# Windowed attention beside a delta rule: from a loop of its own into the levels of the delta steps

## The chip, the cores and the metric

One core of one Trainium2 chip runs the whole program. The metric is the time of one execution in microseconds (us), measured on the device. A core has five engines with an in-order queue each: TensorE (PE: matrix products, and transposes as products with the identity), VectorE (DVE), ScalarE (ACT), GpSimd (POOL) and SyncE (SP), which only issues transfers here. They meet at semaphores only. TensorE writes to PSUM, eight banks of 512 float32 per partition. All numbers are float32; a large product is made of three products of split operands (high and low part), a small one runs in float32 itself, in two passes (so a "x8" in the profile is four matmuls).

## The reference, cut to what matters

Two layers of a transformer trunk over 128 prompt tokens (tile 0) and 512 sample tokens (tiles 1 to 4), 1024 features. The change is in the even layer, whose mixer has two parts side by side behind one input projection and in front of one output projection:

```
s_ctx = einsum("bqgrd,bkgd->bgrqk", q_i, k_ctx) * scale       # window attention of the sample tiles
s_loc = where(valid, einsum("bqgrd,bkgd->bgrqk", q_i, k_i) * scale, -inf)
m = max(max(s), sink); e = exp(s - m); p = e / (sum(e) + exp(sink - m))
oa = p_ctx @ v_ctx + p_loc @ v_i                              # 8 heads of 64, 2 groups of keys
ob, s_f, s_b = delta_bidir(q, k, v, g, beta, s0_f, s0_b)      # 4 heads, forwards and backwards
ob = rmsnorm(ob, out_norm) * silu(gate)
out = concatenate([oa, ob]) @ w_out
```

A prompt tile attends to its own 128 keys. A sample tile attends to its own tile, its neighbours (masked to a window of 128) and 128 cached keys: three key tiles for sample tiles 1 and 4, four for tiles 2 and 3. The reference solves a triangular system per chunk of the delta rule; the kernel does that by doubling.

## The kernel before

The even layer runs in stages. **Input projection**: 23 column blocks of 128, each 48 matmuls; after the last ones the keys and values of the delta rule are turned (`kv_turn`, L2266). **Delta steps** (`for r in range(NT)`, L2390 on PE, L1664 on DVE, L998 on ACT): five steps, each for one tile forwards and one backwards (c = 0 and 1, both in flight), the fifth for the prompt tile. A step makes the decayed Gram matrix, then inverts it in levels: at each level lv = 1 to 5, PE makes Z for both directions (L2418), DVE multiplies Z by that level's mask (`level_z`, L1705), PE makes two products of it ("TR", L2471 and L2474), and DVE adds these into `r_blocks` and `t_blocks` (the level's sums, L1711, L1714). A level needs the sums of the one before. Behind the levels come a last Z and TR (L2496, L2510), V = R times beta v (L2528), the outputs and the new state. Between these, PE has filler: the adaLN map of the other sub-layers, 40 pieces of 1 MB of `w_mod`, whole (L2212) or in two halves (L2221), eight a step, through four buffers (`MSLOTS = 4`), issued by SP, one behind another; the rotation of one of five rows of q and k a step (`rope_swap_a`, L2364, with `rotated_a` on DVE, L1628 to L1636); and `k_times_state` (L2386) at levels 4 and 5, with `v_beta` on DVE (L1661) behind it.

**Attention** (L2612 on PE, L1800 on DVE, L1088 on ACT) starts when the last delta step has ended: 40 units of one tile and one head. Per unit: scores (PE, L2577, two heads at once), scores plus mask and the row maximum in one instruction (DVE, L1806), its negative (L1810), exp with the row sum (ACT, L1095), exp of the sink (L1097), transposes of the probabilities (PE, L2202), their copy (ACT, L500), values (PE, L2600), sum, reciprocal and scaling (DVE, L1785 to L1791). Scores, transposes and values have two PSUM banks each. Between units lie the norm and gate of the delta output (`on_step`, `on_stat`), the split of attention output into high and low part per tile, `gains`, the first two splits of `w_out`, and `keep_busy` (L2207), products that nobody reads. **Output projection** (`out_halves(0)`, L2081) waits for all of it: its first two column blocks have their weights by then, blocks 2 to 7 are split from ACT's `out_split` (L1115) and DVE (L1464) on.

The order on each engine is written out by hand; nothing reorders it.

Of the kernel before, what the change touches and what calls it, by code (L numbers as in the profile page):

```python
# [109 lines left out]
def build(nc, a, outs):  # L110
# [21 lines left out]
    NORMS = (("first", KD, 1), ("l2", 8, 8), ("on", 4, 8), ("cq", C_Q // P, 1), ("ckv", C_KV // P, 1))  # L132
# [162 lines left out]
    MSLOTS = 4  # L295
# [3 lines left out]
    MROW = place("mod_rows", [512], R_T + 4 * al(TW))  # L299
    SM = [place(f"scores{s}", [512], R_F + 1024 + 512 * s) for s in range(2)]  # L300
    PR = [place(f"probs{s}", [512], R_F + 2048 + 512 * s) for s in range(2)]
    PT = [place(f"probs_t{s}", [512], R_F + 3072 + 512 * s) for s in range(2)]
    ASM = place("attn_small", [256], R_F + 4096)
    OA = [place(f"o_attn{s}", [512], R_F + 512 * s) for s in range(2)]
# [154 lines left out]
    ALLU = [(t, c + 4 * g2) for t in ATT for c in range(4) for g2 in range(2)]  # L459
    A_ROPE = (4, 0, 1, 2, 3)  # L460
    ON_AT = [4 + 8 * h for h in range(B_HEADS)]

    def on_head(u, step):

        return ON_AT.index(u - step) if u - step in ON_AT else None
# [26 lines left out]

    def att_copy_a(act, u):

        t, h = ALLU[u]
        c0, c1 = att_local(t)
        act.wait_ge(S("a_turned"), u + 1)
        if u >= 2:
            act.wait_ge(S("a_pv"), u - 1)
        act.activation(PT[u % 2][:, c0:c1], PS[:, 1024 + 512 * (u % 2) + c0:1024 + 512 * (u % 2) + c1], ACT.Copy  # L500
                       ).then_inc(S("a_pt"), 1)


# [60 lines left out]
    with stack:  # L564
# [4 lines left out]
        def _(sp):  # L569
# [43 lines left out]
            for n in range(23):  # L613
                if n < E_AB:
                    load(n, ein_v[:, :, (6 + n) * P:(7 + n) * P])
                elif n == E_AB:
                    load(n, ein_v[:, :, 22 * P:22 * P + 16])
                    sp.dma_start(CT[:, C_FOUR, 0:16], consts[:, C_FOUR, 0:16]).then_inc(S("consts_landed"), 16)
                    for dst, name in ((DTB, "ev_dt_bias"), (EAL, "ev_a_log")):
                        src = a[name][0].rearrange("(o d) h -> o (d h)", o=1).broadcast_to([P, 8])  # L620
                        sp.dma_start(dst[:, :], src).then_inc(S("side_landed"), 16)
                elif n < E_QA + 4:
                    load_two(n, [ein_v[:, :, 64 * h:64 * h + 64] for h in (n - E_QA, n - E_QA + 4)])
                else:
                    c = n - E_QA if n < E_GATE else n - 1
                    load(n, ein_v[:, :, c * P:(c + 1) * P])
            sp.dma_start(CT[:, C_AMASK:, :], consts[:, C_AMASK:, :]).then_inc(S("consts_landed"), 16)
# [130 lines left out]
        def _(act):  # L758
# [184 lines left out]
            def k_rows(t):  # L943
                act.wait_ge(S("kv_turned"), 2 * t + 1)
                act.activation(KTOK[:, t, :, :], q4(bank(4 + 2 * (t % 2))), ACT.Copy).then_inc(S("k_tok"), 1)
# [51 lines left out]

            for r in range(NT):  # L998
                for c in range(2):
# [6 lines left out]
                    act.activation(DQ[c][:, :, :], DQ[c][:, :, :], ACT.Exp, scale=-1.0).then_inc(S("d_exp"), 1)  # L1006
                for c in range(2):
# [28 lines left out]
                if r == 0:  # L1036
                    act.wait_ge(S("va_turned"), 2)
                    act.activation(AV[:, 4, :], bank(7, P), ACT.Copy).then_inc(S("v_rows"), 1)
                for c in range(2):
# [11 lines left out]
            o_copy(NT - 1, 0)  # L1051


            def on_step(u):

                h = on_head(u, 0)
                if h is not None:
                    if h == 0:
                        for c in range(2):
                            act.wait_ge(*both("o_done", c, NT))  # L1060
                    if h >= 2:
                        act.wait_ge(*of("stat", "on", 2 * (h - 1)))
                    act.activation(ONSQ[h % 2][:, :], OD[:, h, :], ACT.Square).then_inc(S("norm_sq"), 1)
                for hf in range(2):
                    cs = slice(hf * HW, hf * HW + HW)
                    h = on_head(u, 2 + 2 * hf)
                    if h is not None:
                        act.wait_ge(*of("stat", "on", 2 * h + hf + 1))
                        if h >= 2:
                            act.wait_ge(S("on_gated"), 2 * (h - 1))  # L1070
                        act.activation(ONRL[h % 2][:, cs], bank(7, HW), ACT.Ln, scale=1.0 / P, bias=EPSC[:, 0:1]
                                       ).then_inc(S("norm_ln"), 1)
                    h = on_head(u, 3 + 2 * hf)
                    if h is not None:
                        act.wait_ge(*of("ln", "on", 2 * h + hf + 1))
                        act.activation(ONRL[h % 2][:, cs], ONRL[h % 2][:, cs], ACT.Exp, scale=-0.5).then_inc(S("norm_rstd"), 1)
                h = on_head(u, 8)
                if h is not None:
                    act.wait_ge(S("on_gated"), 2 * h + 2)
                    act.activation(Hh[:, 4 + h, :], OD[:, h, :], ACT.Copy).then_inc(S("on_hi"), 1)  # L1080

            def att_out(i, sem):

                t = ATT[i]
                act.wait_ge(S("oa_turned"), i + 1)
                act.activation(Hh[:, 0:4, TILES[t]:TILES[t] + P], q4(bank(6)), ACT.Copy).then_inc(S(sem), 1)

            for u, (t, h) in enumerate(ALLU):  # L1088
                s = u % 2
                c0, c1 = att_local(t)  # L1090
                act.wait_ge(S("a_max"), u + 1)
                if u >= 2:

                    act.wait_ge(S("a_turned"), u - 1)
                act.activation(PR[s][:, c0:c1], SM[s][:, c0:c1], ACT.Exp, bias=ASM[:, 64 + u:65 + u],  # L1095
                               scale=A_HD ** -0.5, accum_out=ASM[:, 128 + u:129 + u]).then_inc(S("a_exp"), 1)
                act.activation(ASM[:, 192 + u:193 + u], SNK[:, h:h + 1], ACT.Exp, bias=ASM[:, 64 + u:65 + u]  # L1097
                               ).then_inc(S("a_sink"), 1)
                if u >= 1:
                    att_copy_a(act, u - 1)  # L1100
                if u in (2, 3):
                    if u == 2:
                        act.wait_ge(S("mod_done"), KD + MPARTS)
                    hi(N0_EVEN_OUT + u - 2)
                on_step(u)
                if u % 8 == 3 and t != ATT[0]:
                    att_out(ATT.index(t) - 1, "oa_hi")
            att_copy_a(act, len(ALLU) - 1)
            att_out(NT - 1, "oa_hi")
# [45 lines left out]
            act.wait_ge(S("on_lo"), B_HEADS)  # L1155
# [178 lines left out]
        def _(dve):  # L1334
# [261 lines left out]
            step(dve.scalar_tensor_tensor(EB[:, :], EB[:, :], -1.0, BETA[:, :], ALU.mult, ALU.mult), "gates_ready")  # L1596
            w_rest(E_GATE + 2)
            for t in range(NT):
                if t == 2:
                    w_rest(E_GATE + 3)  # L1600
                dve.wait_ge(S("kv_turned"), 2 * t + 2)
                dve.tensor_copy(VTOK[:, t, :, :], q4(bank(5 + 2 * (t % 2)))).then_inc(S("v_tok"), 1)
# [5 lines left out]
            def mod_rows(i):  # L1608

                dve.wait_ge(S("mod_done"), KD * (i + 2))  # L1610
                dve.tensor_copy(MROW[:, :], bank(6)).then_inc(S("mod_rows"), 1)

# [4 lines left out]
            def mod_out(i):  # L1617
# [3 lines left out]
                mod_columns(l, m0 // P, 7, "mod_cols")  # L1621

            def rope_a(r, part):

                dst = QA[:, A_ROPE[r], S0:S0 + SAMPLE]
                if part == 0:
                    dve.wait_ge(S("a_swapped"), r + 1)
                    dve.tensor_tensor(ROTA[:, :], bank(7), CT[:, C_SIN:C_SIN + 4, :].rearrange("p a b -> p (a b)"), ALU.mult  # L1628
                                      ).then_inc(S("a_rotated"), 1)
                elif part == 1:  # L1630
                    dve.tensor_tensor(dst, dst, CT[:, C_COS:C_COS + 4, :].rearrange("p a b -> p (a b)"), ALU.mult
                                      ).then_inc(S("a_cosine"), 1)
                else:
                    dve.wait_ge(S("a_rotated"), r + 1)
                    dve.wait_ge(S("a_cosine"), r + 1)
                    dve.tensor_tensor(dst, dst, ROTA[:, :], ALU.add).then_inc(S("a_roped"), 1)  # L1636
# [18 lines left out]
            def v_minus(r, c):  # L1655
# [6 lines left out]
                last.then_inc(S("v_minus"), 1)  # L1662

            for r in range(NT):  # L1664
# [28 lines left out]
                last.then_inc(S("level_ready1"), 1)  # L1693

# [1140 lines left out]
```

## Time and profile before

| | us |
|---|---|
| median of 3 runs | 1902.68 (1900.95 to 1903.35) |
| the profiled execution, its own time | 1901.23 |
| its span | 1899.4 |
| PE busy | 1808.8 (95%) |
| DVE busy | 988.6 (52%) |
| ACT busy | 816.0 (43%) |
| delta steps, 226 to 435.7: PE, DVE, ACT busy of 209.7 | 187.3, 117.1, 51.5 |
| attention, 435.7 to 530: PE, DVE, ACT busy of 94.3 | 83.1, 65.9, 66.3 |

Start times are counted from the span's start. "Idle before" in brackets is the time that the engine stood idle ahead of the instruction, and who ended it; "issue" means that no semaphore explains it. PEclk 1.00 is TensorE's 2.4 GHz, 0.50 its 1.2 GHz. Matmuls overlap, so for PE the distance between starts says what a group costs.

### The profile page before, as it was taken

How to read it: one execution, taken by the hardware profiler on the slowest of the kernel's cores; microseconds unless marked ns; L12 is line 12 of the kernel's file. 1: busy time of each engine (PE TensorE's matmuls, PEld its weight loads, DVE VectorE, ACT ScalarE, POOL GpSimd, SP SyncE). 2: the span in 40 equal slices, each digit the busy share in tenths (PEclk: the TensorE clock that was granted, in tenths of full speed). 3: DMA queues.
4: the chain of work that ended last, by engine and by line, in shares of the span. 5: the costliest groups of instructions: out<-in, count | busy, mean ns of one | idle time of the engine just before them, and what ended most of it. 6: DMA issues, size and time to landing. Idle time of an engine off the chain costs nothing. (4 is left out here: it accounts for less than half of the span.)

```text
span 1899.4 us, 36570 instructions
## 1 busy us (share of the span) xinstructions
PE 1808.8 (95%) x14803; PEld 1667.0 (88%) x14803; DVE 988.6 (52%) x1838; ACT 816.0 (43%) x1396; POOL 55.8 (3%) x57
## 2 busy tenths in 40 slices
PE   5999989988899999999999999999999999999998
PEld 3999867667799999999999887776899999999997
DVE  4443345656747655235556843344376553355555
ACT  4545422225745544124445654343455442243453
POOL 0000222220000000000000000000000000000000
PEclk9999999999999999999999999999999999999999
DMA  7232376751021222222234311011211232122243
GB/s 289 67 69 57 122 222 214 214 178 57 1 72 45 78 74 86 72 67 74 70 99 140 94 49 31 24 33 31 67 45 56 77 89 78 56 77 77 81 135 117
DMA packets 244627, 170.25 MB, mean 90 GB/s; under 512 B 20922, under 2 KB 231068, under 8 KB 243356
## 3 DMA queue, kind: packets, MB, share of 16 engines
q1 hardware_dynamic: 244508, 168.55, 29.8%
q8 instruction: 88, 1.44, 0.3%
q14 instruction: 31, 0.25, 0.0%
HBM read 165.09 MB, written 3.44 MB: 89 GB/s over the span
## 5 line engine op out<-in xcount | busy, mean ns | idle before, releaser
L769 ACT ACTIVATE w_hi<-w_raw 128x1024 fp32r<-128x1024 f32 (+4 forms) x186 | 197.7, 1063 | 529.2 <-PE ps L2003 416.1
L1351 DVE TENSOR_TENSOR w_lo<-w_raw,w_hi 128x1024 fp32r<-128x1024 f32 (+4 forms) x190 | 233.0, 1227 | 346.9 <-ACT w_hi L769 346.5
L2003 PE MATMUL ps<-h_hi,w_hi 128*128 128x320 f32 x1632 | 373.9, 310 | 4.4 <-ACT conv L1178 2.4
L2003 PE MATMUL ps<-h_hi,w_lo 128*128 128x320 f32 x1632 | 371.8, 309 | 0.0
L2003 PE MATMUL ps<-h_lo,w_hi 128*128 128x320 f32 x1632 | 371.7, 309 | 0.0
L2003 PEld LDWEIGHTS ps<-h_hi,w_hi 128*128 128x128 f32 x1632 | 272.8, 188 | 6.5 <-ACT conv L1178 2.9
L2003 PEld LDWEIGHTS ps<-h_lo,w_hi 128*128 128x128 f32 x1632 | 273.0, 188 | 0.0
L2003 PEld LDWEIGHTS ps<-h_hi,w_lo 128*128 128x128 f32 x1632 | 272.8, 188 | 0.0
L2081 PE MATMUL ps<-g_hi,w_hi 128*128 128x320 f32 x352 | 110.1, 313 | 3.2 <-DVE g_lo L1850 2.0
L2081 PE MATMUL ps<-g_lo,w_hi 128*128 128x320 f32 x352 | 108.8, 309 | 0.0
L2081 PE MATMUL ps<-g_hi,w_lo 128*128 128x320 f32 x352 | 108.8, 309 | 0.0
L1357 DVE SCALAR_TENSOR_TENSOR conv<-u,vec_cols,conv 128x511 f32<-128x511 f32 x200 | 101.3, 548 | 14.4 <-ACT conv L1178 11.6
L1361 DVE SCALAR_TENSOR_TENSOR conv<-u,vec_cols,conv 128x511 f32<-128x511 f32 x200 | 100.7, 546 | 0.0
L2081 PE MATMUL ps<-h_hi,w_out_hi 128*128 128x320 f32 x288 | 90.4, 314 | 0.1
L2081 PE MATMUL ps<-h_hi,w_out_lo 128*128 128x320 f32 x288 | 89.0, 309 | 0.0
L2081 PE MATMUL ps<-h_lo,w_out_hi 128*128 128x320 f32 x288 | 89.0, 309 | 0.0
L1183 ACT ACTIVATE g_hi<-gated 128x640 f32 (+1 forms) x44 | 32.6, 742 | 105.1 <-DVE gated L1848 105.1
L2081 PEld LDWEIGHTS ps<-g_hi,w_hi 128*128 128x128 f32 x352 | 66.1, 188 | 4.5 <-DVE g_lo L1850 2.5
L1178 ACT ACTIVATE conv<-ps,vec_cols 128x640 f32<-128x640 f32 x88 | 69.3, 787 | 0.0
L2081 PEld LDWEIGHTS ps<-g_lo,w_hi 128*128 128x128 f32 x352 | 66.1, 188 | 0.2
L2081 PEld LDWEIGHTS ps<-g_hi,w_lo 128*128 128x128 f32 x352 | 66.1, 188 | 0.0
L1868 DVE COPY f_t<-ps 128x640 f32 (+1 forms) x16 | 13.2, 825 | 98.3 <-PE ps L2003 80.5
(364 smaller groups left out, 3299.6 us busy)
## 6 DMA issues: line engine op xcount, KB each, us to landing
w_raw<-in_ffn_w_up SPq DMA_DIRECT2D x88, 512.0 KB, 3.8
w_mod_raw<-in_w_mod SPq DMA_DIRECT2D x80, 512.0 KB, 4.5
w_raw<-in_ffn_w_down SPq DMA_DIRECT2D x48, 704.0 KB, 4.6
w_raw<-in_ev_w_in SPq DMA_DIRECT2D x18, 512.0 KB, 3.8
w_mod_first<-in_w_mod SPq DMA_DIRECT2D x8, 1024.0 KB, 15.8
w_raw<-in_ev_w_out SPq DMA_DIRECT2D x8, 512.0 KB, 4.7
w_raw<-in_od_w_out SPq DMA_DIRECT2D x8, 512.0 KB, 4.1
w_raw<-in_od_w_kv_up SPq DMA_DIRECT2D x24, 128.0 KB, 2.3
```

What stands on the lines that cost most here:

```text
L769: act.activation(WH[slot][:, 0:k, :], RAW[slot][:, 0:k, :], ACT.Copy).then_inc(w_hi, 1)
L1178: act.activation(halves(Y[b][:, :]), pair(b0 + 2 * slot), ACT.Copy, scale=vcol(v0 + b * FCH, j)).then_inc(evac_a, 1)
L1183: act.activation(row(Gh, j), GP[:, :], ACT.Copy).then_inc(S("g_hi_written"), 1)
L1351: dve.tensor_tensor(WL[slot][:, 0:k, :], RAW[slot][:, 0:k, :], WH[slot][:, 0:k, :].bitcast(F32), ALU.subtract).then_inc(w_lo, 1)
L1357: dve.scalar_tensor_tensor(y[:, c0 + 1:c1], u[:, c0:c1 - 1], w_before, y[:, c0 + 1:c1], ALU.mult, ALU.add).then_inc(S(signal), 1)
L1361: dve.scalar_tensor_tensor(y[:, c0:c1 - 1], u[:, c0 + 1:c1], w_after, y[:, c0:c1 - 1], ALU.mult, ALU.add).then_inc(S(signal), 1)
L1868: dve.tensor_copy(halves(row(F, m)), pair(2 * slot)).then_inc(evac_v, 1)
L2003: last = pe.matmul(out, w_of(k, wi), x_of(k, xi, i), start=(k == 0 and p == 0), stop=(k == ks - 1 and p == 2))
L2081: last = pe.matmul(out, w[wi][:, k, :], x[xi][:, k, tk(g)], start=(k == 0 and p == 0), stop=(k == ks - 1 and p == 2))
```

## The change

- The attention loop is gone. Its work stands in the delta steps: tile r's attention in step r. A sample tile has four pairs of heads (q = 0 to 3, one head of each key group). On PE, pair q's scores are behind level q's TR, its transposes (head by head, both through bank 7) around level q + 2's TR, its values in level q + 3, in front of TR. DVE's `pair_max` for pair q stands behind the sums of level q + 1. The prompt tile is one batch of eight heads in step 0.
- There is one set of score banks (2 and 5), so pair q + 1's scores wait for pair q's maximum. The probabilities are written over the masked scores. Sinks, sums, reciprocals and scaling are done once a tile (`normalise`). TR's results move from banks B and C to A and B.
- `k_times_state` moves from levels 4 and 5 to levels 0 and 1 in steps 1 to 3, with `v_beta`.
- The rotations move into the projection's last blocks (one `rope_swap_a` behind each of blocks 18 to 22), for which the constants are loaded earlier; `kv_turn` has three banks instead of four.
- `MSLOTS` falls from 4 to 3, to make room.
- Behind the steps: the delta output's norm (one root over both halves a head), the splits of eight chunks of the output projection's input, one after another in the order `TAIL`, and the first two column blocks, whose products are interleaved chunk by chunk as these come. `keep_busy` is gone there.

The diff's core, in this order: buffers, ACT in a step, DVE's `pair_max` and its place, PE in a level of steps 1 to 4 (TR lies at the third line of dots), `att_scores`, ACT behind the steps (DVE follows it chunk by chunk).

```diff
-    MSLOTS = 4
+    MSLOTS = 3
+    S_BANK, O_BANK, O_AT = (2, 5), (1, 4), 128
+    TAIL = (0, 1, 2, 4, 3, 5, 6, 7)
...
+                att_exps(r, 0)
+                for q in range(pairs(r)):
+                    att_pt_copy(r, q, 0)
+                    if q + 1 < pairs(r):
+                        att_exps(r, q + 1)
+                    else:
+                        att_sink(r)
+                    att_pt_copy(r, q, 1)
...
+            def pair_max(r, q):
+                p, u = batch(r, q), 8 * r + 2 * q
+                c0, c1 = att_local(r)
+                dve.wait_ge(S("a_scores"), p + 1)
+                if p >= 2:
+                    dve.wait_ge(S("a_turned"), 2 * (p - 1))
+                for g2 in range(2):
+                    last = dve.tensor_tensor_reduce(SM[p % 2][:, g2, c0:c1], PS[:, 512 * S_BANK[g2] + c0:512 * S_BANK[g2] + c1],
+                                                    CT[:, C_AMASK:C_AMASK + 4, :].rearrange("p a b -> p (a b)")[:, c0:c1],
+                                                    1.0, SNK8[:, q + 4 * g2:q + 4 * g2 + 1], ALU.add, ALU.max, ASM[:, u + g2:u + g2 + 1])
+                last.then_inc(S("a_rowmax"), 1)
+                dve.wait_ge(S("a_rowmax"), 5 * r - 2 + q)
+                neg_max(u, 2)
...
+                    if 0 < r < NT - 1 and lv == 1:
+                        v_minus(r, 1)
+                    if r > 0 and lv < 5:
+                        pair_max(r, lv - 1)
...
+                    else:
+                        if lv < 4:
+                            mod_first_half(r, lv + 2)
+                        if lv == 1 and r < NT - 1:
+                            k_times_state(r, 1)
+                        if lv > 2:
+                            for c in range(2):
+                                pe.wait_ge(*both("t_written", c, t0 + lv))
+                            att_values(r, lv - 3)
+                        if lv > 1:
+                            att_turn(r, lv - 2, 0)
...
+                        if lv < 4:
+                            mod_piece(r, lv + 2, halved=True)
+                        if lv > 1:
+                            att_turn(r, lv - 2, 1)
+                        if lv < 4:
+                            att_scores(r, lv)
...
+            def att_scores(r, q):
+                if q:
+                    pe.wait_ge(S("a_rowmax"), 5 * r - 3 + q)
+                else:
+                    for c in range(2):
+                        pe.wait_ge(*(both("kq_copied", c, r + 1) if r < 2 else both("o_done", c, r)))
...
+            on_square(0)
+            att_hi(0)
+            hi(N0_EVEN_OUT)
+            on_square(1)
+            on_root(0)
+            hi(N0_EVEN_OUT + 1)
+            att_hi(1)
+            on_square(2)
+            on_root(1)
+            att_hi(2)
+            on_square(3)
+            on_out(0)
+            att_hi(3)
+            on_root(2)
+            on_out(1)
+            on_root(3)
+            on_out(2)
+            on_out(3)
```

## Rows read from the trace of the kernel before

**Rows 1.** The page: busy time of TensorE, and the transfers of `w_mod`.
```profile
PE 1808.8 (95%) x14803; PEld 1667.0 (88%) x14803; DVE 988.6 (52%) x1838; ACT 816.0 (43%) x1396; POOL 55.8 (3%) x57
...
w_mod_raw<-in_w_mod SPq DMA_DIRECT2D x80, 512.0 KB, 4.5
```

**Rows 2.** Stretches, busy time by engine: projection's end, last TR to `w_out`, blocks 0 and 1.
```profile
200.00:219.00 19.00, 19.00 (x138) 18.99 (x137) 3.12 (x4) 3.82 (x6) 0.00 (x0) 1.00 0.00 1
...
434.40:529.59 95.19, 83.95 (x676) 66.24 (x676) 67.16 (x270) 65.93 (x192) 0.00 (x0) 1.00 0.06 18
529.59:536.70 7.11, 7.11 (x48) 7.11 (x49) 2.69 (x3) 3.49 (x6) 0.00 (x0) 1.00 0.37 110
```

**Rows 3.** Stretches, level 1's TR to V in steps 1, 2, 3, 4 (same columns).
```profile
281.96:306.26 24.30, 21.21 (x574) 15.19 (x571) 12.20 (x43) 1.66 (x4) 3.79 (x4) 0.93 0.74 227
325.11:345.73 20.62, 19.71 (x575) 14.16 (x571) 12.07 (x42) 1.67 (x4) 5.12 (x5) 1.00 0.77 232
365.18:388.69 23.51, 20.34 (x575) 14.27 (x571) 12.05 (x42) 1.66 (x4) 4.50 (x5) 1.00 0.71 223
408.14:428.64 20.50, 18.12 (x559) 12.47 (x555) 10.20 (x34) 1.66 (x4) 4.51 (x5) 1.00 0.51 160
```

**Rows 4.** TensorE in time, step 2, level 2: start, duration, engine, line.
```profile
326.75 1.15 PE L2418 MATMUL ps<-r_blocks,a_blocks 64*64 64x64 f32 x32
327.83 0.64 PE L2221 MATMUL ps<-w_mod_raw,silu_c 128*32 128x256 f32 x8
328.40 0.25 PE L2471 MATMUL ps<-level_z,t_blocks 64*64 64x32 f32 x2
...
329.46 0.64 PE L2221 MATMUL ps<-w_mod_raw,silu_c 128*32 128x256 f32 x8
330.03 1.13 PE L2364 MATMUL ps<-qa_ka_va,consts 128*128 128x512 f32 x2
...
335.45 1.16 PE L2386 MATMUL ps<-state,qkv_b 128*128 128x128 f32 x8
```

**Rows 5.** VectorE in time, the last of the same level's sums.
```profile
329.80 0.28 DVE L1714 TENSOR_TENSOR t_blocks<-t_blocks,ps 128x128 f32<-128x128 f32 x1
```

**Rows 6.** TensorE in time, attention units of four key tiles.
```profile
457.84 0.71 PE L2577 MATMUL ps<-qa_ka_va 64*128 64x128 f32 x8
...
458.93 0.66 PE L2202 MATMUL ps<-consts,probs 128*128 128x128 f32 x4
459.42 1.00 PE L2600 MATMUL ps<-v_attn_tok,probs_t 128*128 128x64 f32 x8
```

**Rows 7.** VectorE and ScalarE in time, units of 512 columns.
```profile
454.62 0.75 DVE L1806 CUSTOM_DVE_ANT_0 scores<-ps,consts,sink_scaled 128x512 f32<-128x512 f32 x1 [1.35 <-issue]
...
455.41 0.15 DVE L1810 TENSOR_SCALAR attn_small<-attn_small 128x1 f32<-128x1 f32 x1
...
455.60 0.72 ACT L1095 ACTIVATE probs<-scores,attn_small 128x512 f32<-128x512 f32 x1 [1.81 <-DVE attn_small L1810]
...
458.18 0.58 ACT L500 ACTIVATE probs_t<-ps 128x512 f32<-128x512 f32 x1
```

**Rows 8.** In time: a whole-row copy on ScalarE; then a group of its lines.
```profile
467.34 0.72 ACT L1080 ACTIVATE h_hi<-o_delta 128x640 fp32r<-128x640 f32 x1
...
L1769 DVE TENSOR_TENSOR h_lo<-o_delta,h_hi 128x640 fp32r<-128x640 f32 x4 | 3.3, 818 | 0.0
...
L1126 ACT ACT_TABLE_LOAD x1 | 1.3, 1283 | 0.0
```

**Rows 9.** TensorE alone: length, busy (instructions), granted clock, DMA share, GB/s.
```profile
282.99:284.99 2.00, 0.00 (x0) 1.00 0.54 152
286.40:289.80 3.40, 3.40 (x80) 0.50 0.67 208
231.00:233.00 2.00, 0.00 (x0) 1.00 0.77 217
...
238.70:245.50 6.80, 5.85 (x116) 0.50 0.65 199
```

## What the change does to the time

> **What bounds the kernel now.** The page first: TensorE is busy for 95% of the span [rows 1], so a stage is read by what PE does in it. The stretches by stage come next. The end of the input projection is solid PE, 19.00 of 19.00 us [rows 2]. The delta steps are nearly so: from level 1's TR to V step 2 takes 20.6 us with 19.7 busy; steps 1, 3 and 4 take 24.3, 23.5 and 20.5 [rows 3]. In time, a level is Z (1.08 us from start to start), half a `w_mod` piece (0.57), TR (1.06) and the other half (0.57), and DVE's sums end 1.6 us after TR began [rows 4, 5]; so a level without more costs 3.3 us, and what is put into it costs its own PE time. Behind the steps, 95.2 us pass from the last delta product to the first product of the output projection, and another 7.1 for that projection's blocks 0 and 1: 102.3 us until block 2 starts [rows 2]. PE, DVE and ACT are there busy for 84, 66 and 67 us: none is full, the units go round a chain PE, DVE, ACT, PE, ACT, PE.
>
> **The tail (gain).** What is left behind the steps hangs on ACT. From the last delta product: output copies to +1.4 us, then on ACT 4 squares, 4 attention chunks, 4 delta chunks (640 columns, about 0.63 apart by the 0.72 of [rows 8]), 2 weight splits (0.95 each) and 4 roots (Ln and Exp with a wait between, 1.45), the last two estimated by their length from the same kind of passes: 2.5 + 2.5 + 2.5 + 1.9 + 5.8 = 15.2 us, to +16.6. The last head's gate (two DVE passes, 0.9 each), its copy (0.7) and its low part (0.82, [rows 8]) come behind its root, which ends at +15.5: +19.9. ACT's splits of block 2 wait for that: table load 1.3 [rows 8], split 1.05, DVE 1.25: block 2 starts at +23.6. PE's blocks 0 and 1, interleaved by chunk, need only 0.9 us behind the last chunk and are hidden in this. 102.1 (to 434.4, the last product's end) less 23.6 is **-78.5**. Bounds: if the chunks come as DVE's queue allows and no faster, +26 (-76); if the roots cost 1.2, +22.5 (-79.6). Behind it the splits of blocks 4 to 7 have a cycle of 6.9 us for two (load 4.7, 1.0, 1.2) against PE's 7.0: no cover is left, no cost yet.
>
> **The projection (loss).** A rotation's product costs PE 1.06 us [rows 4]. Four are moved from the steps to a stage that is solid PE: 4.2; the fifth falls where PE waits for ACT's last evacuation, free. Three banks for `kv_turn` cost two short waits for copies, 0.6. **+4.9**, between 4.2 and 6. The steps' side of this move is in the sums below. DVE's 2 us a rotation lie beside, in a stretch where it is 3.1 of 19.0 busy [rows 2].
>
> **A level with attention, four key tiles (steps 2 and 3).** Per pair PE adds: scores 1.09, two turns 0.49 each, values 2 x 0.91 [rows 6]. All times below from TR's start. DVE is through with the sums at 1.6; `pair_max` is two instructions 0.79 apart [rows 7]: 3.2. PE is through with TR, half piece and turn at 2.1 and waits for the maximum, since there is one set of score banks: 1.1 us idle. Then scores, Z, half piece.
> - Level 2 to 3: 3.2 + 1.09 + 1.08 + 0.57 + values 1.82 + turn 0.49 = 8.2.
> - Level 3 to 4: no half piece, and the values wait for the second turn's copy. That copy stands on ACT behind the next pair's exps: maximum 3.2, its negative 0.15, two exps 0.72 apart, copy 0.58 [rows 7], 0.1 for hand-overs: 5.5. Then 1.82 + 0.49 = 7.8.
> - Level 4 to 5: no scores left. PE has TR, turn, Z until 2.6 and waits for the same copy until 5.5: 2.9 us idle. 7.8.
> - Level 1 to 2: `v_beta` (four products, 1.0 in the same timeline) stands on DVE in front of `pair_max`: maximum at 4.2, PE ready at 1.6: 2.6 us idle. 4.2 + 1.09 + 1.08 + 0.57 + 0.49 = 7.45.
> - Level 5 to V: TR 1.06, turn, last Z 0.61, whole piece 0.9, values, TR 0.61, whole piece 0.9 = 6.4. `normalise` is beside V.
>
> Sum 37.7. In front of level 1's TR stand one `k_times_state` (1.1, [rows 4]) and scores more, and the second `k_times_state`: +3.2; that both left levels 4 and 5 is in the comparison. Step 2: 37.7 + 3.2 - 20.6 = **+20.3**. Step 3 (23.5 before; its own first levels were held by DVE's `o_add`, so only +2.5 in front): **+16.7**.
>
> **Three key tiles (steps 1 and 4).** PE's part times 3/4, maxima 0.66 and exps 0.61 apart, copy 0.47: 6.9 + 7.2 + 6.7 + 6.7 + 5.8 = 33.2, idle 2.3, 1.0, 0.9 and 2.4 us. Step 1: 33.2 + 3.0 - 24.3 = **+11.9**. Step 4 has no `v_beta` (32.2); the first scores wait for `o_add` (+1.0), and `normalise` delays v_new by 0.55 since no `gc_rows` covers it: 32.2 + 1.6 - 20.5 = **+13.3**.
>
> **Step 0 (the prompt).** Scores 1.2, turns 0.9, values 1.8 on PE less the rotation 1.1. The scores and the row maximum fall into two waits of PE for `w_mod`, of which 231.00:233.00 is one and the other ended inside 238.70:245.50 [rows 9]. **+1.0**, between -1 and +4.
>
> **Three `w_mod` buffers.** Eight pieces a step need 8 x 4.5 = 36 us [rows 1]; the steps grow from 44 to some 60. Pieces 3 to 5 of a step are issued when 0 to 2 are used, over 5 us before PE comes to them. **0**; if it binds, 1 to 2 us a step.
>
> **What may come back.** Steps 1, 3 and 4 held waits of PE in the middle of a group, without a semaphore (2.15 us in step 1's TR; 1.0, 1.2 and 1.0 in steps 3 and 4: the difference between [rows 3]'s lengths and step 2's). Taking their lengths from the sums as above treats them as gone. I take half of them to come back: **+3** (0 to +6).
>
> **The clock.** PE idle for 2.0 us, 282.99 to 284.99, was followed by 3.4 us at 0.50 (1.2 GHz), 286.40 to 289.80; the wait that ended inside 238.70:245.50 by 6.8 us at it; idle for 2.0 at 231 by none [rows 9]. A stretch at half clock full of PE work costs half of itself: 1.7 us. In the tail PE is busy for some 9 of 24 us, and the low clock will reach into block 2: 1.5 to 3.4 us, I take **+2.6**. In the steps there are seven waits of 2.3 to 2.9 us (level 1 in steps 1 to 3, level 4 in steps 1 to 4). In the forecast they cost nothing: the one of 2.0 at 231 stands for them.
>
> The Trainium skill (TensorE: Matmul & The Clock Gate, "HAM oscillation — how this bites in real kernels") speaks against that: a kernel that works in bursts shorter than the waits between them begins burst after burst at the low clock. The first and second of those three idle stretches agree, the third does not. By that rule the sum would be that of the first rival.
>
> **Sum.** -78.5 + 4.9 + (1.0 + 11.9 + 20.3 + 16.7 + 13.3 = 63.2) + 3 + 2.6 = **-4.8 us**. From the profiled execution's 1901.2 that is 1896.4; the median of the runs is 1.5 above it, so 1898 for a median.
>
> **Rivals.**
> 1. *The merged steps put PE to sleep* (slower). One score set and one ACT queue make seven waits of 2.3 to 2.9 us, and the clock falls behind them. For: two of three such waits did it. Against: much PE work at full clock stands around each. Seven falls at 1.7 are +11.9: +7, 1910. It decides from the fifth fall on (-4.8 + 8.5 = +3.7); chance 0.32.
> 2. *Three falls* or equal sums elsewhere (each level 0.25 us longer than reckoned, 18 levels): 1903, no change. Chance 0.25.
> 3. *The levels absorb more*: DVE starts on a maximum earlier, the semaphore-less waits fall into the new idle, step 0 stays at its `w_mod` pace: -78.5 + 4.9 + 60 + 1.7 = -12: 1891. This lies on the forecast's side; chance 0.13.
> 4. *The change only moves the chain*: the tail takes as long as the attention did. Excluded by the ACT sum: 15 us, not 95.
>
> **Numbers.** A run of this kernel tells from no change what exceeds 0.2%, 3.8 us. Forecast (-4 to -9; 1894 to 1899) 0.30 and rival 3 give faster 0.43; within 0.2% 0.25; slower 0.32. The likeliest's own range is 1893 to 1900; the range for 8 in 10 reaches from 1889 to 1912, as the two large terms (-78.5, +63.2) each carry 3 us and the falls 12.
>
> **What would show it.** Right: 23 to 24 us from the last delta product to block 2; from V to V (the ends of [rows 3]) 60 us in steps 2 and 3 (39.5 and 43.0 before) and 53 in step 4 (40.0); PE idle at level 4 in front of the values, for 2.4 to 2.9 us, ended by ACT's `probs_t`; and in front of the scores, ended by DVE. Wrong: a granted clock under 0.97 in the steps (rival 1), PE waits for `w_mod` (three buffers), or DVE as what ends most waits before TR, which would say that Z's masks come late.

## The result: 0.57% slower

The changed kernel takes 1912.5 us (median of ten executions, 1907.6 to 1919.4), the kernel before 1902.0 beside it (ten, 1898.7 to 1905.7): the ratio is 1.0057, with a 95% interval of 1.004 to 1.0074. The forecast was 1898, 0.25% faster, and its range ended at 1912: the median lies 0.5 us outside it, and the time moved the other way. The profiled executions stand 10.9 us apart (1912.12 and 1901.23), and this is what the account below adds up to. Throughout, +x is x us more than before.

The page and the stretches of the kernel after. The first row answers to [rows 1]; the next four to [rows 3] (level 1's TR to V in steps 1 to 4); the last is the tail, from the last delta product to block 2, for which before had the second and third row of [rows 2]. Columns as there.

```profile
PE 1812.4 (95%) x14703; PEld 1671.7 (88%) x14703; DVE 970.8 (51%) x1706; ACT 811.1 (42%) x1351; POOL 55.7 (3%) x57
...
292.10:328.46 36.36, 30.84 (x645) 23.60 (x645) 15.74 (x57) 10.43 (x29) 0.76 (x1) 0.91 0.45 139
350.07:392.48 42.41, 35.71 (x682) 27.54 (x681) 16.81 (x57) 12.14 (x29) 2.35 (x3) 0.88 0.39 125
414.17:459.09 44.92, 38.13 (x681) 29.57 (x680) 18.11 (x64) 12.14 (x29) 2.27 (x3) 0.83 0.40 124
480.35:515.79 35.44, 30.92 (x649) 23.77 (x645) 15.35 (x53) 10.43 (x29) 3.58 (x4) 0.90 0.35 109
521.57:545.68 24.11, 15.30 (x72) 11.52 (x71) 18.96 (x27) 20.19 (x29) 0.00 (x0) 0.93 0.22 65
```

The tail did what was forecast: 24.1 us where 102.3 stood. The steps did not. Their lengths, 36.4, 42.4, 44.9 and 35.4, were forecast as 33.2, 37.7, 37.7 and 32.2, and the column to read is the granted clock: 0.91, 0.88, 0.83, 0.90, against 1.00 in three of the four before. PE has the same two groups of waits there as forecast (steps 1 to 4; us in total, times, longest):

```profile
PE ps L2517 <- DVE attn_small L1739: 13.9, 12, 2.4
PE ps L2547 <- ACT probs_t L1027: 9.5, 4, 2.6
```

L2517 is the scores, which wait for the maximum; L2547 the values, which wait for their copy. What the second wait looks like in time, step 2, level 5 (start, duration; PE, then DVE, then ACT):

```profile
375.99 0.66 PE L2311 MATMUL ps<-consts,probs 128*128 128x128 f32 x4
376.57 1.15 PE L2589 MATMUL ps<-r_blocks,a_blocks 64*64 64x64 f32 x32
380.34 1.97 PE L2547 MATMUL ps<-v_attn_tok,probs_t 128*128 128x64 f32 x16 [2.61 <-ACT probs_t L1027]
...
376.33 0.28 DVE L1834 TENSOR_TENSOR t_blocks<-t_blocks,ps 128x128 f32<-128x128 f32 x1
376.53 0.74 DVE L1739 CUSTOM_DVE_ANT_0 probs<-ps,consts,sink_scaled 128x512 f32<-128x512 f32 x1
...
377.99 0.17 DVE L1713 TENSOR_SCALAR attn_small<-attn_small 128x2 f32<-128x2 f32 x1
...
378.19 0.72 ACT L1016 ACTIVATE probs<-probs,attn_small 128x512 f32<-128x512 f32 x1 [2.56 <-DVE attn_small L1713]
...
378.91 0.71 ACT L1016 ACTIVATE probs<-probs,attn_small 128x512 f32<-128x512 f32 x1
...
379.62 0.57 ACT L1027 ACTIVATE probs_t<-ps 128x512 f32<-128x512 f32 x1
```

The second turn of the pair (PE, 375.99) was there to be copied at 376.65. ACT stood idle until 378.19 and did the *next* pair's exponentials first, which hung on the maximum, which stood on DVE behind the sums: 376.53, 377.99, 378.19, 379.62, 380.34 is one chain. And this is what followed four such waits and one in front of the scores (415.89), for TensorE alone (length, busy, granted clock, DMA share, GB/s):

```profile
316.87:318.98 2.11, 0.00 (x0) 1.00 0.00 0
321.20:324.60 3.40, 3.40 (x75) 0.53 0.00 0
377.73:380.33 2.60, 0.00 (x0) 1.00 0.00 0
382.60:389.40 6.80, 6.80 (x98) 0.51 0.00 0
415.89:418.28 2.39, 0.00 (x0) 1.00 0.79 235
418.30:425.10 6.80, 5.92 (x140) 1.00 0.67 218
440.46:443.06 2.60, 0.00 (x0) 1.00 0.00 0
444.00:460.80 16.80, 16.80 (x154) 0.50 0.23 69
...
502.62:504.72 2.10, 0.00 (x0) 1.00 0.00 0
505.40:512.20 6.80, 6.80 (x102) 0.50 0.01 2
```

Four waits of 2.1 to 2.6 us, and 0.5 to 2.2 us behind the end of each up to 16.8 us of solid PE work at 1.2 GHz; the fifth was followed by none. With the low clock behind the other two level-1 waits (3.4 us each) it is 41 us at half clock in steps 1 to 4, against 3.4 before.

### The profile page after: what moved, and what is told of

Its sections match the earlier page's. It is cut to its first block and busy times, and to the rows that moved or that the text cites. A ratio compares the mean times of both kernels' runs of the same rounds, so it can differ in the third digit from the quotient of the medians.

```text
span 1910.3 us, 36045 instructions
## 1 busy us (share of the span) xinstructions
PE 1812.4 (95%) x14703; PEld 1671.7 (88%) x14703; DVE 970.8 (51%) x1706; ACT 811.1 (42%) x1351; POOL 55.7 (3%) x57
## 5 line engine op out<-in xcount | busy, mean ns | idle before, releaser
L1222 ACT ACTIVATE g_hi<-gated 128x640 f32 (+1 forms) x44 | 32.6, 741 | 104.9 <-DVE gated L1935 104.9
## 6 DMA issues: line engine op xcount, KB each, us to landing
w_mod_first<-in_w_mod SPq DMA_DIRECT2D x8, 1024.0 KB, 15.9
```

The costliest lines, as they stand in the source:

```text
L1222: act.activation(row(Gh, j), GP[:, :], ACT.Copy).then_inc(S("g_hi_written"), 1)
```

## Experiments

**Is it the clock, or the waits themselves?** Theory C: the low clock. Theory W: the waits and longer chains. The filler adds zeros to a sum that is open anyway, so it changes no value. The diff is shortened.

```diff
+def add_zero(n, b=6):     # PE: zero column times identity, added to mod's open group
+    for _ in range(n):
+        pe.matmul(bank(b, P), ZEROC[:, 0:1].broadcast_to([P, P]), const(C_ID), start=False, stop=False)
 ...                       # in att_scores(r, q)
+if q == 1 and 0 < r < NT - 1: add_zero(7)
 pe.wait_ge(S("a_rowmax"), 5 * r - 3 + q)
 ...                       # level 5, r > 0
+add_zero(8)
 pe.wait_ge(*both("t_written", c, t0 + lv))
 att_values(r, lv - 3)
```

> The changed kernel with products that add zero (a zero column times the identity, 128x128 f32, about 0.28 us each) put into PE's seven waits of 2.1 to 2.6 us: seven in front of the scores of level 1 in steps 1 to 3, eight in front of the values of level 5 in steps 1 to 4. No wait is shortened: PE is only busy in it. Theory C (the low clock is what the steps cost beyond the forecast): the stretches at 0.50 between 285 and 515 us, 41.8 us of them in the changed kernel, go nearly all; as PE was busy through most of them, the time falls by 12 to 18 us, to about 1897 (ratio to the kernel before 0.997). Theory W (the waits themselves and longer chains on DVE and ACT cost it, and the low clock falls into them): the time stays within 2 us of 1912, ratio 1.005. V to V in step 3 is 66.6 us now: under C 58 to 60, under W 66.

Measured: 1895.2 us, ratio 0.9965 (0.995 to 0.9981). The 17.4 us came from giving PE useless work; by the two ratios it is 0.92%, 17.5 us. The same four stretches as above, and the filler in the wait of step 2's level 5:

```profile
292.43:326.09 33.66, 31.71 (x675) 25.02 (x674) 15.74 (x57) 10.45 (x29) 0.78 (x1) 1.00 0.48 152
347.70:385.75 38.05, 35.06 (x712) 28.37 (x711) 16.80 (x57) 12.16 (x29) 2.36 (x3) 1.00 0.44 137
407.44:445.58 38.14, 35.05 (x711) 28.36 (x710) 17.27 (x60) 12.15 (x29) 2.28 (x3) 1.00 0.44 136
465.96:498.60 32.64, 29.96 (x665) 23.40 (x661) 15.39 (x53) 10.45 (x29) 3.62 (x4) 1.00 0.40 120
...
373.83 2.05 PE L2508 MATMUL ps<-consts,zero 128*128 128x128 f32 x16
376.51 0.74 PE L2557 MATMUL ps<-v_attn_tok,probs_t 128*128 128x64 f32 x5 [0.64 <-ACT probs_t L1029]
```

Clock 1.00 in all four, and lengths of 33.7, 38.1, 38.1 and 32.6 where the forecast had 33.2, 37.7, 37.7 and 32.2. Theory C holds: the time fell by what it said, and step 3 takes 59.8 us from V to V, inside its 58 to 60. The forecast's arithmetic of the levels was right at full clock.

**Which waits?** Two halves of a_fill (without one or the other `add_zero`), and one with three and four products instead of seven and eight, f_half, which ran before the two halves.

> a_fill (1895.2 us) without its filler in front of the scores of level 1: only the four waits in front of the values of level 5 are filled, the three of 2.1 to 2.4 us at level 1 stay. If the seven waits cost alike (17.4 us over seven, 2.5 each): 1902.6. If the level-5 waits are the dear ones, as the stretches at 0.50 behind them say (34 of 41 us in the changed kernel, 10.2 of f_half's steps against none behind its level-1 waits): 1897 to 1899.

> The other half: only the three waits in front of the scores of level 1 are filled, the four of level 5 stay. Alike: 1905. Level-5 waits dear: 1908 to 1911.

> As a_fill (the changed kernel with products that add zero in PE's seven waits; 1895.2 us, no stretch at 0.50 left in steps 1 to 4), with three and four products instead of seven and eight: some 0.8 and 1.1 us of work, so 1.3 to 1.6 us of idle PE are left of each wait. If what matters is that no idle stretch of 2 us and more is left, the time is a_fill's, 1895 to 1897, with no 0.50 in the steps. If the clock falls for what PE does around a wait as a whole, shortening the wait by half takes away half of the falls: 1902 to 1905.

Measured: j_fill5 1897.9 us (0.9995, 0.9985 to 1.0006), k_fill1 1911.5 (1.007, 1.0047 to 1.0093), f_half 1901.3 (1.0007, 0.9987 to 1.0028). The waits in front of level 5's values are the dear ones: filling them alone brings 10 to 15 us (the lower figure against the changed kernel as it ran beside, 1907.7 us), filling the level-1 waits alone nothing that can be told, and on top of the others 0.3%. f_half came between its two expectations, nearer to the second. Its level-1 waits (1.3 to 1.5 us left) were followed by no low clock, three of its four level-5 waits by 20.4 us of it, one of them only 1.0 us long. First the wait of step 2 and what followed it, then step 4's, which had 2.1 us of PE work at full clock between it and the fall:

```profile
372.12:373.62 1.50, 0.00 (x0) 1.00 0.00 0
374.20:384.20 10.00, 10.00 (x113) 0.50 0.01 2
...
493.90:494.90 1.00, 0.00 (x0) 1.00 0.00 0
...
497.00:500.40 3.40, 3.40 (x83) 0.50 0.00 0
```

So the length of the idle time alone doesn't decide. What sets level 5 apart stays open.

**How far does it repeat?**

> The changed kernel itself once more, for how far its stretches at 0.50 repeat. The time is 1910 to 1914. If each fall is fixed by the instructions around it, the same six of seven waits are followed by the same 3.4, 3.4, 3.4, 6.8, 17.1 and 6.8 us at 0.50; if the fall depends on where a wait lies in time against what the throttle looks at, the same seven waits stay and the stretches behind them differ in number and length, with 30 to 50 us in all.

Measured: 1907.7 us (1904.7 to 1920.8), ratio 1.0048 (1.0035 to 1.0061); its profiled execution was the longest of the nine. All seven waits are there with the same lengths, all seven are followed by low clock, 54 us of it, and the stretches are others than above. Behind step 1's level-5 wait, which had 3.4 us in the other profile:

```profile
319.40:321.50 2.10, 0.00 (x0) 1.00 0.00 0
323.40:337.00 13.60, 13.60 (x138) 0.50 0.32 101
```

Over the profiles of the changed kernel (two), b_copy, d_lv1, j_fill5 and k_fill1, 15 of 16 unfilled level-5 waits were followed by low clock, 8.5 us on average, and 9 of 12 at level 1, by 3.1. The executions of the changed kernel scatter too, over 12 and 16 us. Each of its 19 executions has a mean clock; (1 - clock) x 2 x span is its time at 1.2 GHz, 38 to 73 us, and a line through the 19 gives 0.46 us of execution for each us of that, and, drawn on past the points, 1887 at none. The same line meets the kernels that have the changed kernel's waits, filled or not, and another clock. Line first, then the measured mean of all executions: k_fill1 1911.2 and 1911.4, f_half 1902.5 and 1902.9, j_fill5 1897.4 and 1897.6, a_fill 1894.2 and 1895.4. The clock explains the scatter and what the fillers gained with one price.

**What makes the waits, and are they needed?** Three edits, shortened here: the order of ACT's queue, level 1's order, and the place of the maximum.

```diff
 # b_copy (ACT)
 att_pt_copy(r, q, 0)
+att_pt_copy(r, q, 1)
 if q + 1 < pairs(r): att_exps(r, q + 1)
 else: att_sink(r)
-att_pt_copy(r, q, 1)
 # d_lv1 (PE: k_times_state(r, 1) from ahead of level 1's TR to behind its half piece; DVE:)
+pair_max(r, 0)
 v_minus(r, 1)
-pair_max(r, 0)
 # c_max (DVE, levels 1 to 4)
 ZS[c] = masks
+pair_max(r, lv - 1)
 RB[c], TB[c] += sums
-pair_max(r, lv - 1)
```

> The changed kernel with one edit on ACT: the copy of a pair's second turned half comes ahead of the next pair's two exponentials, not behind them. It no longer waits for the next maximum, so the values of levels 4 and 5 find their probabilities ready: PE's waits there (2.1 to 2.6 us at level 5 in four steps, 9.5 us in all) fall under 0.5 us each. The exponentials come 0.6 us later, in front of a turn that PE reaches later still. Theory W: the four waits and about as much at level 4 go, 9 to 12 us less, 1901. Theory C: as the four waits are also what put the clock down (34 us at 0.50 behind them), another 12 to 17 us go: 20 to 28 us less, 1885 to 1892. If the copy is not what the values wait for: no change.

> The changed kernel with level 1 reordered in steps 1 to 3: the second k_times_state comes on PE behind TR and the half piece (into the wait for the maximum) instead of ahead of TR, and its v_beta pass stands on DVE behind the maximum instead of ahead of it. Theory W: the wait of 2.1 to 2.4 us goes, half of it filled by 1.1 us of work, half since the maximum comes 1 us earlier: 3 x 2.1 = 6 us less, 1906. Theory C: the falls behind these waits go too (297.2, 355.0; the one at 415.9 was followed by none): 3.4 us more, 1902 to 1903, while the falls behind the level-5 waits stay.

> The changed kernel with the edits of b_copy and d_lv1 together; the maximum stays behind the sums. Neither a wait of 2 us nor a filler is in it. V to V from a_fill's 58.0, 59.7, 59.8 and 53.0 us less the level-1 wait (2.1 us in steps 1 to 3) and the level-4 and level-5 waits for the copy (2.2 to 2.6 us): 53.5, 55, 55 and 50.8, with no 0.50; 16 us under a_fill, 1879. Rival, that the maximum behind the sums itself keeps the levels apart beyond PE's idle time (so that c_max has its 40 us from the sums' place and not from waits): steps stay at 57 or more, 1888.

> The changed kernel with the masked maximum where the description of the change says it is not: on DVE between a level's masks and its sums. The maximum ends then 1.7 us after TR began instead of 3.2, the sums 3.3 instead of 1.6. If the maximum behind the sums is what makes PE wait (13.9 us in front of the scores, 2.4 us at level 1), most of these waits go and the exponentials come 1.6 us earlier: 10 to 15 us less, and with the three level-1 waits their falls of the clock: 1895 to 1900. Rival: the sums now come last in front of Z; a level with DVE's masks, maximum and sums in a row costs PE 0.2 to 1 us more at each of 16 levels, and the time rises by 3 to 15 us.

The kernel before took 1901.4 us beside the first set of these kernels (a_fill, b_copy, c_max, d_lv1), 1900.6 beside the second (f_half, g_both, h_maxcopy, i_maxfill) and 1898.5 beside the third; the ratios are what compares over sets, and the sums below are good to some 3 us.

Measured: b_copy 1891.3 us (0.9941, 0.9922 to 0.996), d_lv1 1904.9 (1.0018, 0.9994 to 1.0042), g_both, which is both, 1879.3 (0.9866, 0.9835 to 0.9897), c_max 1872.0 (0.9849, 0.9814 to 0.9884). Two parts add up to each: PE's waits that go, and the low clock behind them. g_both: the 9.5 us of waits for the copy, 6.4 of the 13.9 for the maximum (7.5 are left, none over 1.1) and the 17.4 of a_fill are 33.3, measured 33.2 by the medians and 36.3 by the ratios. c_max: 9.5 + 13.9 + 17.4 = 40.8, measured 40.5 and 39.6. The line of above gives the first part by itself: b_copy, d_lv1, g_both and c_max lie 8.2, 6.9, 15.4 and 23.1 us under it, and their profiles have 9.5, 6.7, 15.9 and 23.4 us less of the two waits than the changed kernel.

Of the expectations, b_copy's under theory C (1885 to 1892) and g_both's (1879) came true. d_lv1 lies between its two, and ten executions over 17.7 us can't tell them apart. c_max's (1895 to 1900) missed by over 20 us: it left the waits for the copy standing, took for the clock only the falls of level 1, and its rival feared for the sums. The four stretches of c_max:

```profile
290.59:320.42 29.83, 28.67 (x646) 21.83 (x645) 15.38 (x53) 10.44 (x29) 0.77 (x1) 1.00 0.55 169
342.03:373.08 31.05, 31.02 (x682) 24.86 (x681) 15.71 (x55) 12.03 (x29) 2.34 (x3) 1.00 0.52 166
394.77:426.07 31.30, 31.27 (x681) 25.04 (x680) 16.90 (x58) 12.04 (x29) 2.27 (x3) 1.00 0.52 163
446.45:474.27 27.82, 27.69 (x648) 21.53 (x644) 15.03 (x53) 10.45 (x29) 3.59 (x4) 1.00 0.46 140
```

PE is busy for 31.0 of 31.1 us in step 2. Its level 2 in time (DVE's last maximum and negative and last sum, then PE's turn, scores and Z):

```profile
346.96 0.74 DVE L1739 CUSTOM_DVE_ANT_0 probs<-ps,consts,sink_scaled 128x512 f32<-128x512 f32 x1
...
347.75 0.17 DVE L1713 TENSOR_SCALAR attn_small<-attn_small 128x2 f32<-128x2 f32 x1
...
348.43 0.28 DVE L1836 TENSOR_TENSOR t_blocks<-t_blocks,ps 128x128 f32<-128x128 f32 x1
...
348.63 0.66 PE L2311 MATMUL ps<-consts,probs 128*128 128x128 f32 x4
349.21 0.72 PE L2517 MATMUL ps<-qa_ka_va 64*128 64x128 f32 x8
...
350.31 1.15 PE L2589 MATMUL ps<-r_blocks,a_blocks 64*64 64x64 f32 x32
```

The maximum is through 1.3 us before PE wants to write the next scores, and the sums, though later, 1.6 us before Z reads them: DVE's two passes lie beside TR instead of behind it.

**What is left to take.** On top of c_max: b_copy's order too (h_maxcopy), fillers in step 0 and in the tail (i_maxfill), and h_maxcopy without a load of ACT's table (m_noload).

```diff
 # i_maxfill, step 0 and tail
+if u == 1: add_zero(8)                     # ahead of the wait for w_mod piece 1
+add_zero(5, 1); ... add_zero(10, 1)        # tail, into a bank that nothing reads there
 # m_noload, out_proj(i)
-act.preload_act_table_set("natural_log_exp_and_others")
+if i: act.preload_act_table_set("natural_log_exp_and_others")
```

> c_max (the maximum between masks and sums, 1872.0 us) with b_copy's order on ACT. In c_max's profile PE waits nowhere in the steps for a maximum or for a copy of probabilities, so the second edit has nothing to remove: 1872 within 2 us. If the copies still hold something that is not listed as a wait (a PSUM bank, the turns), up to 3 us less.

> c_max with products that write nothing of use in the waits that are left outside the steps: eight in step 0's wait for the w_mod piece 1 (2.5 us, 6.8 us at 0.50 behind it), and in the tail 5, 3, 3, 4 and 10 (before block 2 PE is idle for 3.2 us, with 3.4 us at 0.50 behind it and as much at the tail's begin). If PE sets the pace behind each: 3.4 us less in step 0 and 1.7 in block 2, 1867. If step 0 goes at the pace of the w_mod transfers, only the block 2 part: 1870. A tail that goes round ACT gets nothing from a faster PE before block 2.

> h_maxcopy (1871.6 us) without the load of ACT's table ahead of the first output projection: the table has been in place since the delta steps began. The load takes 1.28 us on the chain between the last copy of the tail and block 2's split, so block 2 starts 1.3 us earlier and the time is 1870.3. If the block waits for its weights' low part or a bank instead, under 0.5 us. Against the kernel before either is faster by 1.5 to 1.8%.

Measured: 1871.6 (0.983, 0.9798 to 0.9861), 1870.7 (0.9823, 0.9792 to 0.9854) and 1872.1 us (0.9866, 0.9842 to 0.9889): none can be told from c_max. That was h_maxcopy's expectation; i_maxfill fits its second case (1870, step 0 at its own pace) as well as no gain at all, and m_noload's 1.3 us do not show. In i_maxfill step 0 ran at full clock and took 40.2 us from its first product to V, c_max 40.3 with 6.8 us at half clock in it: PE doesn't set its pace. That the `w_mod` transfers do fits the expectation, but no run changed them. In m_noload block 2 did start earlier, 23.4 us behind the last product instead of h_maxcopy's 24.5, and PE then waited for f_t 1.4 us before a later block: the gain went into the next wait. The waits of PE for f_t behind the last product, h_maxcopy first (c_max has the same), then m_noload:

```profile
PE ps L2168 <- ACT f_t L813: 3.2, 1, 3.2
```

```profile
PE ps L2169 <- ACT f_t L813: 3.3, 2, 1.9
```

c_max is the version to keep: one line of the changed kernel moved, 1.5% faster than before and 2.1% faster than the change as it was made.

## Why the prediction was wrong

By its own terms, in us of the profiled executions:

- **The tail, -78.5: right.** 24.11 us against the 23.6 forecast, -78.2 (102.3 less 24.11; the forecast took 102.1 once). One sum in it doesn't add up as printed: 15.5 with two passes of 0.9, a copy of 0.7 and a low part of 0.82 is 18.8 and not 19.9. The trace has the root's end at +15.5 and the low part's at +19.8: DVE comes to the last gate 0.9 us after the root, as it is still at the low part before it. The figure was right, and one of its terms was not printed.
- **The projection, +4.9: right within 1.** The first product of the steps starts at 226.06 instead of 220.24: +5.8.
- **Step 0, +1.0: right.** First product to V: 41.67 us against 40.34, +1.3.
- **The steps at full clock, +62.2: right.** From the first V to the last one a_fill takes 230.5 us, the kernel before 168.1: +62.5. The waits had their places, releasers and lengths: 2.1 to 2.4 at level 1 (forecast 2.3 and 2.6) and 2.1 to 2.6 at level 5 (2.4 to 2.9; the prediction's "level 4 to 5"). Step by step it is +12.3, +20.2, +16.9 and +13.1 against the 11.9, 20.3, 16.7 and 13.3 forecast.
- **Waits without a semaphore that come back, +3: none did.** The 62.5 leave 0.3 for them.
- **Three `w_mod` buffers, 0: right.** No wait for a piece in steps 1 to 4.
- **The clock in the tail, +2.6: nearly.** 3.4 us at 0.50 reach into block 2, +1.7 if half of it is lost; those inside the tail lie where PE waits for ACT and DVE.
- **"In the forecast they cost nothing": the step that failed.** From the first V to the last the changed kernel takes 248.1 us, 17.5 more than a_fill, which has the same waits; the medians say 17.4. With these the four steps grew by 79.9 us, where 62.2 and the 3 were forecast: 14.7 over.

Sum: -78.2 + 5.8 + 1.3 + 79.9 + 1.7 = +10.5 of the 10.9 measured; 0.4 was not traced. a_fill, in which that one term is taken out, stands at 1896.2 in its profiled execution; the forecast for one was 1896.4. That this is within 0.2 us is partly luck: the terms as measured, without the clock in the steps, are -6.9, 1894.3.

So rival 1, *the merged steps put PE to sleep*, is what happened, and it had a chance of 0.32 and a price of 11.9. Two things were off. The forecast took the wait at 231 (2.0 us, no fall) to stand for seven, against two waits of three that said otherwise [rows 9]. The rule quoted from the Trainium skill (TensorE: Matmul & The Clock Gate, "HAM oscillation — how this bites in real kernels") stood with the two, but its condition, work shorter than the waits between, is not what the change made: step 2 has 35.7 us of PE work in 42.4, and its longest wait is 2.6. The low clock came all the same. And the price of a fall was taken from the shorter of the two low stretches on record, 3.4 us. The other was 6.8 [rows 9], and the seven waits had 5.8 us of low clock each on average (41 over 7): 2.5 us a wait by a_fill, not 1.7. So even the rival's +7 is 3.9 short of the 10.9: its falls were 5.6 too cheap, and the 3 us that did not come back made up for half of that.

Rival 3 (the levels absorb more) was wrong: at full clock the steps took what the forecast said. One part of it came true, since the waits without a semaphore did not come back. The last condition, DVE in front of TR, did not come up either.

## What to carry to other kernels

Where new waits of PE of some 2 us stand in an otherwise solid stretch, charge each with half of the low clock behind it, at its mean length on record, and say what fills or removes it, before believing a sum that is 5 us from no change. An instruction that only feeds a later stage (a maximum, an exponential) belongs on its queue where the queue waits anyway, here between masks and sums while PE does TR, and never ahead of a copy that PE already waits for. To tell the price of a wait from the price of the clock behind it, fill the wait with work of no use: its length stays and only the clock changes.

## What the runs showed of the hardware

- The low clock can outlast its wait by far: 2.6 us idle in step 3, then 16.8 us at 1.2 GHz with PE busy for all of it.
- The fall is not a function of the wait's length alone: 2.4 us idle at 415.89 was followed by none, 1.0 us at 493.90 in f_half by 3.4 us of it.
- A microsecond at half clock in a stretch that is PE's cost 0.46 us of execution, over 19 executions of one kernel with 38 to 73 us of it each.
- Products that add zero to an open accumulation group, 0.26 us each (eight in 2.05 us), kept the clock at 1.00 in steps 1 to 4 of a_fill's profile, and the time fell by 17 us.
- Executions scatter with such waits: ten of the changed kernel over 11.9 us and ten of d_lv1 over 17.7, against 6.5 for ten of a_fill and 4.2 for ten of j_fill5. It is not theirs alone: the kernel before took 7.0 for ten, and among 24 later ones had single executions of 1909.4 and 1911.0 us at a mean clock of 0.992 and 0.993, where most are at 0.995 to 0.998.
